# Two-phase MLPs in seven half-size products, with the activations kept in DRAM between the phases

## The chip, the cores and the metric

One core of a Trainium2 chip runs the whole program in one launch. The metric is the device time in microseconds (us), 2476.63 as the median of three runs (2475.12 to 2477.98). Engine names are those of the profile: PE is TensorE, DVE is VectorE, ACT is ScalarE, POOL is GpSimd, SP is SyncE, which only issues DMAs here.

## The reference

Two layers (gated linear attention, then sliding-window attention), each followed by the same kind of MLP, for 1024 prompt tokens and 64 sample tokens, which the kernel treats as 1088 columns. All values are float32. Only the two MLPs are touched by the change:

```python
D_MODEL = 1024
D_FF = 4 * D_MODEL
...
def squared_relu_mlp(h, w_up, w_down):
    return jnp.square(jax.nn.relu(h @ w_up)) @ w_down
...
        h = rms_norm(x, norm_g[i, 2])
        x = x + rms_norm(squared_relu_mlp(h, mlp_w_up[i], mlp_w_down[i]), norm_g[i, 3])
```

## The kernel before

Everything lies with features on the 128 partitions and the 1088 tokens (`T`) along the free axis; `HALF_T` is 544. Each float32 product is made of three fp32r passes: operands are split in a high part (a cast by ACT) and a low part (value minus high part, by DVE or POOL), and PE adds hi·hi, hi·lo and lo·hi (`dense`, `dense_set`). A unit of weights is 128x1024 (512 KB); SP loads it in a slot of `w_raw`, ACT writes `w_hi`, POOL writes `w_lo` over the raw values.

The MLP has 32 tiles of 128 hidden features, in eight groups of four. For each group the kernel makes the four up tiles (`up_tile`, 72 matmuls each, out of 8 tiles of `h`), takes relu, times the norm factor `keep`, squares, and multiplies by the group's rows of the down weights, adding into `y` in SBUF. In groups 1 to 6 the down product is done as Winograd's form of Strassen's scheme: the operands are cut in two by two blocks, and seven products of half size (`PRODUCTS`, A11, S3, S1, ... are the left operands, the weight sides are differences that `mix` makes) take the place of eight. One pass `p` of four makes the output tiles p and p+4 in 7 products of 12 matmuls with 272 columns each. DVE reads each product out of PSUM and adds it to `y` (`take_product`), makes the sums of activations (`add`), their low parts (`low`) and the weight differences of the next pass (`mix`). ACT casts high parts (`high_pair` for weights) and squares. POOL writes the two low parts of a pass's weights (`low_pair`: 768 and 1024 columns), each after the differences are there.

The first group of an MLP (`for b in range(NB): for j in range(FF_TILES)`) runs block by block of tokens (384, 384, 320 columns) because the norm before it (`Border`) is finished block by block meanwhile; I call it the first wave. The last group's down product runs block by block too, for the norm after it; that is the end wave. Every engine has its own queue in program order, and the order is written by hand; semaphores count what has been done.

Of the kernel before, what the change touches and what calls it, by code (L numbers as in the profile page):

```python
# [7 lines left out]
F32 = mybir.dt.float32  # L8
# [6 lines left out]
P = 128  # L15
# [51 lines left out]
class Chip:  # L67


    def __init__(self, nc, ctx, units):  # L70
        self.nc, self.ctx = nc, ctx
        self.end = (nc.sbuf_base + 31) // 32 * 32
        self.h_hi = self.place("h_hi", [P, KT, T], F32R)
        self.h_lo = self.place("h_lo", [P, KT, T], F32R)
        self.y = self.place("y", [P, KT, T])
        self.keep = self.place("keep", [P, T])
# [16 lines left out]
        self.x_dram = nc.dram_tensor("x_scratch", [P, KT, T], F32, kind="Internal").ap()  # L93

# [33 lines left out]
class WeightStream:  # L128

    def __init__(self, chip, units):
        self.chip, self.units = chip, units
        self.raw_in = [chip.sem(f"w_raw_in{s}") for s in range(SLOTS)]
# [3 lines left out]
        self.finished = 0  # L138

# [16 lines left out]

    def hi_count(self, unit):
        return unit + 1 - 4 * self.groups_before(unit)

    def up_raw_count(self, u0, i, g):  # L160

        per_group = 3 if i % 2 else 1
        return self.raw_count(u0 + i) + 2 - per_group * PAIRED.start + per_group * g

    def up_hi_count(self, u0, i, g):
        return self.hi_count(u0 + i) + 8 - 4 * PAIRED.start + 4 * g

    def pair_number(self, u0, p, g):
        return PAIRS * (self.groups_before(u0) - PAIRED.start) + p + PAIRS * g

# [3 lines left out]
    def load(self, sp, unit):  # L174

        s = unit % SLOTS
        sp.wait_ge(self.used, self.slots_before(unit) - SLOTS + 1)
        sp.dma_start(self.chip.w_raw[:, s], self.units[unit]).then_inc(self.raw_in[s], 16)

    def load_rounds(self, sp, first, end):  # L180

        extra = 4 * self.groups_before(SLOTS * first)
        with sp.Fori(first, end) as i:
            for s in range(SLOTS):
                sp.wait_ge(self.used, SLOTS * i + (s - SLOTS + 1 + extra))
                sp.dma_start(self.chip.w_raw[:, s], self.units[SLOTS * i + s]).then_inc(self.raw_in[s], 16)

    def load_groups(self, sp, u0):

        self.load_rounds(sp, u0 // SLOTS + 1, u0 // SLOTS + 2)  # L190
        self.load(sp, u0 + 8)
        before, first = self.group_slots_before(u0), u0 + 9 - 8 * PAIRED.start
        with sp.Fori(PAIRED.start, PAIRED.stop) as g:
            for n in range(FF_TILES):
                s = (n + 1) % SLOTS
                sp.wait_ge(self.used, 12 * g + (before + n - SLOTS + 1))
                sp.dma_start(self.chip.w_raw[:, s], self.units[8 * g + (first + n)]).then_inc(self.raw_in[s], 16)
            for p in range(PAIRS):
                s = self.pair_slots(p)[0]
                sp.wait_ge(self.used, 12 * g + (before + FF_TILES + 2 * p - SLOTS + 1))  # L200
                sp.dma_start(self.chip.w_raw[:, s], self.units[8 * g + (first + FF_TILES + p)]).then_inc(self.raw_in[s], 16)
        for unit in range(u0 + 8 * PAIRED.stop + 1, u0 + MLP_UNITS):
            self.load(sp, unit)

    def group_slots_before(self, u0):
        return self.slots_before(u0) + 9 - 12 * PAIRED.start

    def pair_slots(self, p):

        return (1, 2) if p % 2 == 0 else (3, 0)  # L210

    def high_of(self, act, s, landed):
        act.wait_ge(self.raw_in[s], landed)
        self.chip.nc.scalar.copy(self.chip.w_hi[:, s], self.chip.w_raw[:, s]).then_inc(self.hi_done, 1)  # L214

    def low_of(self, pool, s, highs):
        c = self.chip
        pool.wait_ge(self.hi_done, highs)
# [3 lines left out]
    def high(self, act, unit):  # L222

        self.high_of(act, unit % SLOTS, 16 * self.raw_count(unit))

    def low(self, pool, unit):

        self.low_of(pool, unit % SLOTS, self.hi_count(unit))

    def high_up(self, act, u0, i, g):  # L230
        self.high_of(act, i, 16 * self.up_raw_count(u0, i, g))

    def low_up(self, pool, u0, i, g):
        self.low_of(pool, i, self.up_hi_count(u0, i, g))

# [2911 lines left out]
```

## Time and profile before

| what | us |
|---|---|
| median of three runs | 2476.63 |
| the profiled execution, whole | 2476.98 |
| its span, first to last instruction | 2475.2 |
| PE busy with matmuls | 2419.3 |
| DVE busy | 1240.9 |
| ACT busy | 935.3 |
| POOL busy | 626.4 |

The mean granted TensorE clock was 0.992 of full speed. The span is what the trace shows, and the whole time has 1.8 us more around it. Busy times overlap, so the engines' rows don't add up to the span; a busy PE says that a matmul was in flight, not that no cycle was lost.

### The profile page before, as it was taken

To read this page: it belongs to the slowest core of one execution; us is meant where nothing else is said; L and a number is where in the kernel's file an instruction comes from. 1 tells how busy PE (TensorE), PEld (TensorE's weight loads), DVE (VectorE), ACT (ScalarE), POOL (GpSimd) and SP (SyncE) were. 2 spreads that over 40 slices of the span, in tenths; PEclk is the share of its full clock that TensorE was granted. 3 is DMA by queue.
4 is the path that set the end of the run, shared out by engine and by line. 5 is a ranking of instruction groups with operands and counts; after the bars stand their busy time and mean duration, and the time that the engine had idled before them with its cause. 6 is when DMAs were issued, how large, how long until landed. Compare 5 with 4: busy or idle time off the path is not lost.

```text
span 2475.2 us, 45129 instructions
## 1 busy us (share of the span) xinstructions
PE 2419.3 (98%) x18094; PEld 2289.4 (92%) x18094; DVE 1240.9 (50%) x2325; ACT 935.3 (38%) x1826; POOL 626.4 (25%) x352
## 2 busy tenths in 40 slices
PE   8999999999999999999999999999999999999998
PEld 8888887799999999999999877699999999999997
DVE  6554455418245545545548344516435455445546
ACT  5454544527222232232226455536412322322222
POOL 0101020116213223322326101014313223233233
PEclk9999999999999999999999999899999999999999
DMA  3101011015111011111115100014211111111024
GB/s 113 44 18 51 19 42 41 22 47 167 60 35 60 31 45 59 42 34 59 51 47 161 62 27 19 31 35 135 75 43 44 34 59 51 34 51 59 26 80 132
DMA packets 62725, 139.03 MB, mean 56 GB/s; under 512 B 8544, under 2 KB 39520, under 8 KB 62592
## 3 DMA queue, kind: packets, MB, share of 16 engines
q1 hardware_dynamic: 54720, 130.51, 16.3%
q10 hardware_dynamic: 7808, 6.56, 0.9%
q8 instruction: 94, 1.54, 0.3%
q14 instruction: 39, 0.32, 0.0%
q0 software_dynamic: 64, 0.10, 0.0%
HBM read 117.74 MB, written 19.40 MB: 55 GB/s over the span
## 4 chain that ended last, share of the span: by engine, by line
PE 88%; DVE 6%; ACT 3%; issue 2%; ACTq 0%; POOL 0%; DVEq 0%; POOLq 0%
PE banks L326 32%; PE banks L310 22%; PE banks L1176 20%; PE banks L2242 4%; PE banks L2377 1%; PE banks L2396 1%; DVE y L753 1%; DVE norm_acc_x L713 1%; PE banks L1752 1%; PE banks L1733 1%; PE banks L1720 1%; PE banks L1760 1%; ACT banks L625 1%; PE banks L2386 1%; DVE norm_acc L702 1%
## 5 line engine op out<-in xcount | busy, mean ns | idle before, releaser
L219 POOL TENSOR_TENSOR w_lo<-w_raw,w_hi 128x1024 fp32r<-128x1024 f32 x116 | 285.5, 2466 | 1036.4 <-ACT w_hi L214 1036.0
L310 PE MATMUL banks<-h_hi,w_hi 128*128 128x384 f32 (+1 forms) x1224 | 423.3, 346 | 4.7 <-DVE h_lo L2807 2.1
L310 PE MATMUL banks<-h_lo,w_hi 128*128 128x384 f32 (+1 forms) x1224 | 404.6, 331 | 0.0
L310 PE MATMUL banks<-h_hi,w_lo 128*128 128x384 f32 (+1 forms) x1224 | 404.2, 330 | 0.0
L266 POOL TENSOR_TENSOR w_lo<-w_raw,w_hi 128x768 fp32r<-128x768 f32 x96 | 202.4, 2129 | 638.9 <-DVE w_raw L252 638.9
L1402 DVE TENSOR_TENSOR y<-banks,y 128x544 f32<-128x544 f32 x336 | 243.3, 724 | 201.8 <-PE banks L1176 197.4
L326 PE MATMUL banks<-h_hi,w_hi 128*128 128x384 f32 (+1 forms) x1368 | 301.9, 329 | 2.0 <-DVE y L1402 2.0
L326 PE MATMUL banks<-h_lo,w_hi 128*128 128x384 f32 (+1 forms) x1368 | 301.3, 328 | 0.0
L326 PE MATMUL banks<-h_hi,w_lo 128*128 128x384 f32 (+1 forms) x1368 | 301.3, 328 | 0.0
L310 PEld LDWEIGHTS banks<-h_hi,w_hi 128*128 128x128 f32 x1224 | 232.0, 190 | 27.3 <-issue 19.3
L326 PEld LDWEIGHTS banks<-h_hi,w_hi 128*128 128x128 f32 x1368 | 233.5, 188 | 2.4 <-issue 2.4
L326 PEld LDWEIGHTS banks<-h_hi,w_lo 128*128 128x128 f32 x1368 | 233.8, 188 | 0.0
L326 PEld LDWEIGHTS banks<-h_lo,w_hi 128*128 128x128 f32 x1368 | 233.7, 188 | 0.0
L310 PEld LDWEIGHTS banks<-h_lo,w_hi 128*128 128x128 f32 x1224 | 232.5, 190 | 1.3
L310 PEld LDWEIGHTS banks<-h_hi,w_lo 128*128 128x128 f32 x1224 | 231.7, 189 | 0.0
L214 ACT CAST w_hi<-w_raw 128x1024 fp32r<-128x1024 f32 x132 | 137.9, 1046 | 189.7 <-DMA w_raw<-in_units 188.8
L1176 PE MATMUL banks<-mlp_a_hi,w_hi 128*128 128x272 f32 x768 | 158.5, 288 | 0.0
L1176 PE MATMUL banks<-mlp_a_lo,w_hi 128*128 128x272 f32 x768 | 158.4, 288 | 0.0
L1176 PE MATMUL banks<-mlp_a_hi,w_lo 128*128 128x272 f32 x768 | 158.2, 288 | 0.0
L1367 DVE SCALAR_TENSOR_TENSOR mlp_a_raw<-banks,keep 128x768 f32<-128x768 f32 (+1 forms) x60 | 40.7, 720 | 209.1 <-PE banks L326 209.1
L2884 DVE COPY_PREDICATED gla_att<-gla_masks,banks 128x128 f32<-128x128 uint8 (+1 forms) x108 | 31.8, 295 | 176.5 <-PE banks L2362 174.1
L1176 PEld LDWEIGHTS banks<-mlp_a_lo,w_hi 128*128 128x128 f32 x768 | 120.3, 189 | 0.0
(238 smaller groups left out, 4481.9 us busy)
## 6 DMA issues: line engine op xcount, KB each, us to landing
w_raw<-in_units SPq DMA_DIRECT2D x180, 512.0 KB, 3.5
x_scratch<-y SPq DMA_DIRECT2D x48, 192.0 KB, 2.6
norm_x<-x_scratch SPq DMA_DIRECT2D x28, 192.0 KB, 3.3
x_scratch<-y SPq DMA_DIRECT2D x24, 160.0 KB, 1.8
norm_x<-x_scratch SPq DMA_DIRECT2D x20, 160.0 KB, 2.9
y<-in_x SPq DMA_DIRECT2D x16, 192.0 KB, 4.9
out_y<-y SPq DMA_DIRECT2D x16, 192.0 KB, 3.3
norm_x<-in_x SPq DMA_DIRECT2D x12, 192.0 KB, 3.2
```

The costliest lines, as they stand in the source:

```text
L214: self.chip.nc.scalar.copy(self.chip.w_hi[:, s], self.chip.w_raw[:, s]).then_inc(self.hi_done, 1)
L219: c.nc.gpsimd.tensor_tensor(c.w_lo[:, s], c.w_raw[:, s], c.w_hi[:, s].bitcast(F32), ALU.subtract).then_inc(self.ready, 1)
L266: c.nc.gpsimd.tensor_tensor(c.w_lo[:, s, at], c.w_raw[:, s, at], c.w_hi[:, s, at].bitcast(F32), ALU.subtract).then_inc(self.pair_ready, 1)
L310: mm = chip.nc.tensor.matmul(out, w, x, start=(first and n == 0), stop=(last and n == 2))
L326: mm = chip.nc.tensor.matmul(chip.banks[:, bank0 + b, 0:WIDTH[b]], w, x[:, k, COLS[b]], start=(k == 0 and n == 0), stop=(k == n_k - 1 and ...
L625: nc.scalar.activation(out, y, ACT.Square).then_inc(self.s.squared_x, 1)
L702: self.chip.nc.vector.tensor_tensor(acc, before, square, ALU.add).then_inc(self.s.summed, 1)
L1176: mm = nc.tensor.matmul(chip.banks[:, bank + c, 0:half], w, x[:, c * half:(c + 1) * half], start=(not prod.adds and kappa == 0 and n == 0) ...
L1367: op = nc.vector.scalar_tensor_tensor(out=out, in0=bank, scalar=0.0, in1=keep, op0=ALU.max, op1=ALU.mult)
L1402: nc.vector.tensor_tensor(y, self.slot_banks(self.PRODUCTS[i].slot), y, ALU.add).then_inc(self.prod_added, 1)
L2242: mm = nc.tensor.matmul(out, x, y, start=(k == 0 and i == 0), stop=(k == KT - 1 and i == 2))
L2884: nc.vector.copy_predicated(a, self.masks[0:n, i, 0:n], chip.banks[0:n, self.X_BANK, i * P:i * P + n]).then_inc(self.att_step if i < 2 els ...
```

## The change

Each MLP now runs in two phases. First all 32 up tiles: four in the first wave as before, two more plain ones, and 26 in 13 "doubles", each of which makes two tiles by seven half-size products of 24 matmuls (four pairs of input tiles deep). For that the sums of `h` are made in SBUF after the first wave (`sums_of_h`, with `gain` on ACT). What a double gives has to be put together by DVE (`C22_TWO` to `C21_TAKEN`), and the sums for the second phase are made at once (`sums_of_act`). Four activation blocks and three sums are stored to DRAM (`store_set`, 1088 KB and 816 KB for a set of two tiles). Then the second phase: seven groups of four passes over the stored sets, all in seven half-size products, with operands loaded back in seven pieces of 544 KB a group (`load_piece`), cast by ACT (`high_piece`) and split by DVE (`low_piece`, two halves of 544 columns). The four first tiles' down product is the end wave. Both `mix` calls of a double and the one of a pass are on DVE; POOL keeps `low_pair`. The sums overwrite what was the raw operand, and two weight units of a double lie in the memory of `y`, which is free in the first phase. The loops of DVE, ACT, POOL and SP are written out; PE's are loops over two doubles, and over two groups.

```diff
-    def tensor(self, pe): ...
+        double(0, 0, first=True)
+        with pe.Fori(1, (DOUBLES + 1) // 2) as r:
+            double(2 * r + -1, 1)
+            double(2 * r, 0)
+        down(0, 0, first=True)
+        with pe.Fori(1, (GROUPS + 1) // 2) as r:
+            down(2 * r + -1, 1)
+            down(2 * r, 0)
...
+        def down_bank(d, i):
+            before, n = {0: (1, 4), 1: (1, 5), 2: (1, 7), 3: (0, 1), 4: (0, 2), 5: (1, 6), 6: (0, 3)}[i]
+            pe.wait_ge(self.y_added, self.adds(d + -before, n))
...
+        def double_until_c21(n):
+            c22, banks, last = self.halves(self.c22[:]), self.slot_banks, n == DOUBLES - 1
+            dve.wait_ge(self.copied, self.copies(n + 1))
+            full(n, 1)
+            combine(n, self.C22_TWO, self.c22[:], banks(1), c22, ALU.add)
+            full(n, 2)
+            combine(n, self.C22_THREE, self.c22[:], banks(2), c22, ALU.add, self.C22_TWO)
+            ws.mix(dve, nc.vector, self.down_unit(0) if last else self.double_unit(n + 1, 0))
+            if last:
+                low_piece(0, 0)
+            full(n, 3)
+            dve.wait_ge(self.a_out, self.outs(n + 1))
+            nc.vector.scalar_tensor_tensor(out=self.halves(a11), in0=banks(3), scalar=0.0, in1=self.halves(keep[0]),
+                                           op0=ALU.max, op1=ALU.mult).then_inc(self.stepped, 1)
+            if last:
+                low_piece(0, 1)
+                low_piece(0, 2)
+            else:
+                ws.mix(dve, nc.vector, self.double_unit(n + 1, 1))
+            full(n, 5)
+            combine(n, self.C22_FULL, self.c22[:], banks(5), c22, ALU.add, self.C22_THREE)
+            combine(n, self.C12_RAW, a12, c22, banks(4), ALU.subtract, self.C22_FULL)
+            relu(n, a12, a12, 0, self.C12_RAW)
+            relu(n, a22, self.c22[:], 1, self.C22_FULL)
+            if last:
+                low_piece(0, 3)
+            full(n, 6)
+            combine(n, self.C21_RAW, a21, c22, banks(6), ALU.subtract)
+            relu(n, a21, a21, 1, self.C21_RAW)
...
+        for d in range(PAIRS * GROUPS):
+            g, p = divmod(d, PAIRS)
+            for i in range(self.N_PROD):
+                take_product(d, i)
+                if i == 1 and d < PAIRS * GROUPS - 1:
+                    ws.mix(dve, nc.vector, self.down_unit(d + 1))
+                if d == 0 and i < 3:
+                    low_piece(0, 4 + i)
+                if g < GROUPS - 1:
+                    piece = {(1, 2): 0, (1, 5): 1, (2, 1): 2, (2, 3): 3, (2, 5): 4, (3, 2): 5, (3, 5): 6}.get((p, i))
+                    if piece is not None:
+                        low_piece(g + 1, piece)
```

How the queue of DVE moved is best seen in its instructions. At the end of the first wave (the 320-column block) it had these before (`mlp_a_raw<-banks` takes a tile out of PSUM, `mlp_a_lo` is its low part, `y<-banks` comes from the first down product):

```order
L1354 SCALAR_TENSOR_TENSOR mlp_a_raw<-banks,keep 128x320
L1345 TENSOR_TENSOR mlp_a_lo<-mlp_a_raw,mlp_a_hi 128x384
L1354 SCALAR_TENSOR_TENSOR mlp_a_raw<-banks,keep 128x320
L1345 TENSOR_TENSOR mlp_a_lo<-mlp_a_raw,mlp_a_hi 128x320
L1354 SCALAR_TENSOR_TENSOR mlp_a_raw<-banks,keep 128x320
L1345 TENSOR_TENSOR mlp_a_lo<-mlp_a_raw,mlp_a_hi 128x320
L1354 SCALAR_TENSOR_TENSOR mlp_a_raw<-banks,keep 128x320
L1345 TENSOR_TENSOR mlp_a_lo<-mlp_a_raw,mlp_a_hi 128x320 x2
```

In the changed kernel the same place has four sums of `h` (`mlp_s_raw`) between one tile and the next:

```order
L1619 SCALAR_TENSOR_TENSOR mlp_first_act<-banks,keep 128x320
L1502 SCALAR_TENSOR_TENSOR mlp_s_raw<-y,gains,mlp_s_raw 128x544
L1504 SCALAR_TENSOR_TENSOR mlp_s_raw<-y,gains,mlp_s_raw 128x544
L1507 TENSOR_TENSOR mlp_s_raw<-mlp_s_raw 128x544
L1509 TENSOR_TENSOR mlp_s_raw<-mlp_s_raw 128x544
L1619 SCALAR_TENSOR_TENSOR mlp_first_act<-banks,keep 128x320
```

So each tile is taken out of PSUM behind the four sums of the tile before it, and the low parts of the first tiles have gone to the end of the MLP.

Before the first double, DVE has this queue (`h_lo` and `mlp_s_lo` are low parts of the sums, `mlp_act<-banks` takes a plain tile; the first product of the double is to be written in the first plain tile's PSUM banks):

```order
L240 TENSOR_TENSOR w_raw<-w_raw 128x512
L243 TENSOR_TENSOR w_raw<-w_raw 128x256
L245 TENSOR_TENSOR w_raw<-w_raw 128x256
L240 TENSOR_TENSOR wide_raw_57<-wide_raw_57 128x512
L243 TENSOR_TENSOR wide_raw_57<-wide_raw_57 128x256
L245 TENSOR_TENSOR wide_raw_57<-wide_raw_57 128x256
L1513 TENSOR_TENSOR mlp_s_lo<-mlp_s_raw,mlp_s_hi 128x1632 x4
L1542 SCALAR_TENSOR_TENSOR mlp_act<-banks,keep 128x768
L1542 SCALAR_TENSOR_TENSOR mlp_act<-banks,keep 128x320
L1513 TENSOR_TENSOR h_lo<-mlp_s_raw,h_hi 128x544 x4
L1542 SCALAR_TENSOR_TENSOR mlp_act<-banks,keep 128x768
```

Before the change there were only copies of the down product in this place:

```order
L1407 COPY y<-banks 128x768
L1407 COPY y<-banks 128x320
L1407 COPY y<-banks 128x768
L1407 COPY y<-banks 128x320
L1407 COPY y<-banks 128x768
```

What is new there is the four wide subtractions and two sets of weight differences, in front of the first plain tile's reading.

In a pass of the down phase DVE had takes of products (`y<-banks,y`) and the three weight differences (`w_raw`), with register arithmetic of the loop between:

```order
L1402 TENSOR_TENSOR y<-banks,y 128x544
L244 ISA
L245 REGISTER_ALU
L247 TENSOR_TENSOR w_raw<-w_raw 128x512
L249 ISA
L250 TENSOR_TENSOR w_raw<-w_raw 128x256
L251 REGISTER_ALU
L252 TENSOR_TENSOR w_raw<-w_raw 128x256
L1399 REGISTER_ALU
L1400 REGISTER_ALU
L1402 TENSOR_TENSOR y<-banks,y 128x544
```

In the changed kernel, from the differences of the second pass of a group (p = 1) to those of the third:

```order
L240 TENSOR_TENSOR w_raw<-w_raw 128x512
L243 TENSOR_TENSOR w_raw<-w_raw 128x256
L245 TENSOR_TENSOR w_raw<-w_raw 128x256
L1603 TENSOR_TENSOR y<-banks,y 128x544
L1513 TENSOR_TENSOR h_lo<-h_raw,h_hi 128x2x544
L1603 TENSOR_TENSOR y<-banks,y 128x544 x3
L1513 TENSOR_TENSOR h_lo<-h_raw,h_hi 128x2x544
L1603 TENSOR_TENSOR y<-banks,y 128x544 x3
L240 TENSOR_TENSOR w_raw<-w_raw 128x512
```

Two low parts of loaded pieces (`h_lo<-h_raw`) now stand between the takes, one of them two places behind the differences.

## Rows read from the trace of the kernel before

**Rows 1.** Chain that ended last, MLP 0: start us, us, what

```profile
624.07 10.57 PE banks L310 x72
...
635.27 12.24 PE banks L326 x72
647.61 96.23 PE banks L326 x576
743.85 41.94 PE banks L1176 x336
785.78 48.00 PE banks L326 x288
...
1236.45 36.24 PE banks L326 x216
1272.68 21.20 PE banks L310 x120
```

**Rows 2.** What PE waited for: us in total, times, longest

```profile
PE banks L519 <- DVE norm_acc_x L713: 3.1, 3, 1.4
```

**Rows 3.** Groups by shape, 744 to 1235 us: busy us, mean ns | idle before

```profile
L1402 DVE TENSOR_TENSOR y<-banks,y 128x544 f32<-128x544 f32 x167 | 121.0, 724 | 100.1 <-PE banks L1176 97.9
...
L266 POOL TENSOR_TENSOR w_lo<-w_raw,w_hi 128x1024 fp32r<-128x1024 f32 x23 | 55.3, 2406 | 0.0
...
L266 POOL TENSOR_TENSOR w_lo<-w_raw,w_hi 128x768 fp32r<-128x768 f32 x23 | 42.6, 1852 | 298.9 <-DVE w_raw L252 298.9
L259 ACT CAST w_hi<-w_raw 128x1024 fp32r<-128x1024 f32 x23 | 24.3, 1055 | 46.7 <-DVE w_raw L252 46.7
...
L1292 ACT CAST mlp_late_s_hi<-mlp_s_raw 128x544 fp32r<-128x544 f32 x30 | 19.5, 650 | 3.3
```

**Rows 4.** Groups by shape on DVE, 620 to 745 us

```profile
L1416 DVE TENSOR_TENSOR y<-y 128x2176 f32<-128x2176 f32 x2 | 4.8, 2424 | 0.0
```

**Rows 5.** DVE in order of time in a paired pass: start us, us, instruction

```profile
847.40 0.72 DVE L1402 TENSOR_TENSOR y<-banks,y 128x544 f32<-128x544 f32 x1 [0.77 <-PE banks L1176]
848.04 0.68 DVE L247 TENSOR_TENSOR w_raw<-w_raw 128x512 f32<-128x512 f32 x1
848.76 0.42 DVE L250 TENSOR_TENSOR w_raw<-w_raw 128x256 f32<-128x256 f32 x1
849.22 0.42 DVE L252 TENSOR_TENSOR w_raw<-w_raw 128x256 f32<-128x256 f32 x1
```

**Rows 6.** POOL in order of time, the same pass

```profile
849.81 4.22 POOL L266 TENSOR_TENSOR w_lo<-w_raw,w_hi 128x768 fp32r<-128x768 f32 x2 [6.26 <-DVE w_raw L252]
```

**Rows 7.** POOL in order of time, in the first wave

```profile
584.12 2.31 POOL L768 TENSOR_TENSOR y<-y,norm_x 128x384 f32<-128x384 f32 x2
...
590.29 2.02 POOL L768 TENSOR_TENSOR y<-y,norm_x 128x384 f32<-128x384 f32 x2 [1.91 <-DVE y L753]
...
630.15 2.40 POOL L219 TENSOR_TENSOR w_lo<-w_raw,w_hi 128x1024 fp32r<-128x1024 f32 x1 [12.11 <-ACT w_hi L214]
```

**Rows 8.** DVE in order of time, in the first wave

```profile
584.55 1.00 DVE L787 SCALAR_TENSOR_TENSOR h_lo<-y,gains,h_hi 128x384 fp32r<-128x384 f32 x1
...
595.36 0.61 DVE L787 SCALAR_TENSOR_TENSOR h_lo<-y,gains,h_hi 128x384 fp32r<-128x384 f32 x1
...
624.56 0.49 DVE L1354 SCALAR_TENSOR_TENSOR mlp_a_raw<-banks,keep 128x320 f32<-128x320 f32 x1 [1.36 <-ACT keep L648]
...
628.04 0.48 DVE L1345 TENSOR_TENSOR mlp_a_lo<-mlp_a_raw,mlp_a_hi 128x320 fp32r<-128x320 f32 x1
...
631.56 1.34 DVE L1345 TENSOR_TENSOR mlp_a_lo<-mlp_a_raw,mlp_a_hi 128x320 fp32r<-128x320 f32 x1
```

**Rows 9.** DMA issues: KB each, median us from issue to landing

```profile
w_raw<-in_units SPq DMA_DIRECT2D x180, 512.0 KB, 3.5
x_scratch<-y SPq DMA_DIRECT2D x48, 192.0 KB, 2.6
```

**Rows 10.** Stages: us, busy (x) of PE, PEld, DVE, ACT, POOL, clock, DMA share, GB/s

```profile
744.00:1236.00 492.00, 491.45 (x3455) 491.23 (x3454) 255.77 (x389) 133.85 (x159) 149.66 (x68) 1.00 0.15 47
```

More of the change, by code:

```diff
@@ L180, in load_rounds @@
     def load_rounds(self, sp, first, end):
-        extra = 4 * self.groups_before(SLOTS * first)
+        shift = self.plain(SLOTS * first) - SLOTS * first
         with sp.Fori(first, end) as i:
             for s in range(SLOTS):
-                sp.wait_ge(self.used, SLOTS * i + (s - SLOTS + 1 + extra))
+                sp.wait_ge(self.used, SLOTS * i + (s - SLOTS + 1 + shift))
                 sp.dma_start(self.chip.w_raw[:, s], self.units[SLOTS * i + s]).then_inc(self.raw_in[s], 16)
[L188 to L203, printed above, removed]
@@ new lines, in double @@
+        def double(n, parity, first=False):
+            places = ((2, 4), (5, 0))[parity]
+            weights = [(places[k // 2], k % 2) for k in range(KT // 2)]
+            pair0 = 2 * ws.pair(self.double_unit(0, 0))
+            for i in range(self.N_PROD):
+                double_bank(n, i, first)
+                if i < 2:
+                    pe.wait_ge(ws.pair_ready, 4 * n + (pair0 + i + 1))
+                if first and i == 2:
+                    pe.wait_ge(self.a_ready, self.operands(KT // 2))
+                if first and i == 1:
+                    pe.wait_ge(self.a_ready, self.operands(KT // 2 + 1))
+                steps = product(i, range(KT // 2), weights)
+                for k in steps:
+                    if i < 2 and k == 1:
+                        pe.wait_ge(ws.pair_ready, 4 * n + (pair0 + 2 + i + 1))
+                    if first and i == 1 and k < KT // 2 - 1:
+                        pe.wait_ge(self.a_ready, self.operands(KT // 2 + k + 2))
@@ new lines, in scalar @@
+        for k in range(KT // 2):
+            act.wait_ge(self.stepped, self.steps(4 * k + 4))
+            nc.scalar.copy(self.s_hi[:, self.row(k)], self.s_raw[:, self.row(k)]).then_inc(self.a_hi_done, 1)
+        for part in range(2):
+            ws.high_pair(act, self.double_unit(0, part))
+        act.wait_ge(self.stepped, self.steps(self.PLAIN_STEP + 1))
+        tiles = [self.act[:, 2 * j:2 * j + 2] for j in range(PLAIN_TILES)]
+        square(tiles[0])
+        act.wait_ge(self.prod_full, self.plains(PLAIN_TILES))
@@ L1455, in vector @@
[L1455 removed]
+                if b == NB - 1:
+                    sums_of_h(j)
+        for part in range(2):
+            ws.mix(dve, nc.vector, self.double_unit(0, part))
+        for k in range(KT // 2):
+            r = self.row(k)
+            low(self.s_lo[:, r], self.s_raw[:, r], self.s_hi[:, r], self.operands(k + 1))
+        take_plain(0)
+        for k in range(KT // 2):
+            low(self.operand(self.S3, k, chip.h_lo, None), self.s3_raw[:, k], self.operand(self.S3, k, chip.h_hi, None),
+                self.operands(KT // 2 + k + 1))
```

903 lines of the change are left out of this document (495 added, 408 removed).

## The prediction

> **What bounds the kernel now.** I read the page first: PE is busy for 2419.3 of the span's 2475.2 us (the table above). Then the chain of work that ended last, in order of time, through MLP 0 [rows 1]: from the end of the first wave (634.64) to the start of the end wave (1272.68) there are 638.0 us, nearly all in unbroken pieces of PE. MLP 1 repeats this. So only what shortens PE's own work, or makes it wait, can count. Two rates are to be seen: four up tiles (288 matmuls of 363 columns on average) take 48.00 us, 12.0 a tile; one group's down product in half-size products (336 matmuls of 272 columns) takes 41.94, 124.8 ns each. Per column both are 0.46 ns, so a half-size product costs PE what its columns say. The other engines have room on average (DVE 255.8 of 492 us in groups 1 to 6, POOL 149.7) [rows 10], and the question is when, not how much.
>
> **What PE saves.** 26 up tiles took 26 x 12.0 = 312.0 us; 13 doubles of 7 x 24 = 168 matmuls take 13 x 20.97 = 272.6. The first group's plain down product (48.0) becomes a seventh group of 41.94. The stretch from first wave to end wave is then 24.0 (two plain tiles) + 272.6 + 7 x 41.94 = 590.2 us if PE never waits, 47.8 less than now. Ahead of the stretch PE waited 1.4 us for the norm sums in each MLP [rows 2]; DVE and ACT lose a low part and a cast per tile there (about 0.5 us each, eight times), so I give that wait back too.
>
> **Prices of what is added.** A take of 544 columns is 0.724 us [rows 3]; back to back it is 0.64, since ends overlap as the next instruction's start shows [rows 5]. From 544 and 2176 columns (2.424) [rows 4] a DVE subtraction costs 1.04 ns a column and 0.16 fixed: 1.29 us for a loaded piece (1088), 1.86 for a wide one (1632). The three weight differences take 1.6 us in all (848.04 to 849.64) [rows 5]. ACT: 544 columns 0.65, 1024 1.06, so 1.11 for a piece [rows 3]. POOL's two low parts: 1.85 and 2.41 [rows 3].
>
> **Where DVE and POOL meet.** In the first wave a DVE instruction with both inputs in SBUF does not run beside one of POOL: the 320-column subtraction takes 0.48, but 1.34 at 631.56, while POOL runs from 630.15 to 632.55 [rows 7, 8]: it waits for POOL's end. The 384-column one takes 0.61 alone and 1.00 at 584.55, and POOL's pair beside it 2.31, not 2.02: DVE got in between POOL's two, and POOL waited for it [rows 7, 8]. So they take turns, and a turn can last 2.4 us. Takes (one input in PSUM) are not touched: POOL's 4.22 us pair from 849.81 [rows 6] lies beside several takes. Before the change, the paired passes had only takes beside POOL's work; now sums, relus, pieces and differences (all SBUF on SBUF) stand there. This is what I price. The Trainium skill says the same in SBUF — State Buffer, Who interferes with whom: a DVE instruction with two SBUF inputs and a GpSimd instruction that reads SBUF exclude each other for the whole instruction, whoever is first. By that rule the trace agrees; a sum that ignored it would be the second rival below.
>
> A steady pass of the down phase (p = 1 or 3). The second product is ready 3.1 us after the pass begins, differences are done at 5.5 (POOL began at 849.81, the pass at 844.27) [rows 1, 6]. ACT then casts the second weight half (1.05) and the piece (1.11): ready at 7.7. POOL started its second, long operation at 7.35 and holds DVE until 9.7; piece 1.29, then take of product 3 until 11.7. The next pass's first product wants that bank at 10.5: PE waits 1.3. With the second piece, product 2 of the next pass waits a little too: 1.5 in all. For p = 2 the piece stands right behind the differences, DVE is first, POOL waits 1.0 and then 1.1 for the second piece, and the second weight half is 0.2 late. With its takes, 0.3. A group loses 1.5 + 1.5 + 0.3 = 3.3 us; groups 1 to 5: 16.5.
>
> The last group has four pieces of first tiles and two subtractions more per pass (0.72 each, `turn_back`) in the same places: I carry the queues on in the same manner and get 7.5.
>
> Start. With W the end of the first wave: the first 320-column tile is taken at W-9.6 (624.56 + 0.49) [rows 8]. ACT squares it and makes three scaled copies (0.75 each as an estimate from the 0.65 of a cast, 0.66 in a row), done W-7.0; DVE makes four sums (2.7) and only then takes the next tile, at W-3.7, not W-6.5. Again ACT (W-1.1, cast of the first plain unit until W-0.1), POOL's low part until W+2.7, into which two of DVE's sums run (2.2 us wait), the third tile is taken at W+4.4. The plain tile needs it and begins 4.4 late (0.6 before). Later DVE makes differences (3.2), then four wide low parts (7.4) against POOL's four weight operations (8.5), in turns; the first plain tile is read behind them at W+33.0, while PE has ended both at W+28.4 and needs its banks: 4.6. Another 0.6 in the first double. Start: 9.6.
>
> The doubles. 21 us each, DVE has 12.6 of work, POOL 8.5; the tightest need is the second unit's low part at 22.5, made at about 19 to 21. No wait. It holds if the stores land: 1904 KB are issued about 4 and 6 us into a double and have to be there at 18 (22.5 less POOL's 1.85, the differences' 1.6 and the relu's 0.7). At the rate of the trace (47 GB/s at a share of 0.15, 313 at full share) [rows 10] they need 6.2 us and the fixed part: 512 KB landed in 3.5 [rows 9], 1.7 of it transfer, so 1.8. They land at about 13.
>
> Between the phases, double 12 and group 0: the pieces must be cast and split between the combining steps. Piece 0 waits for POOL (2.0), the block C21 is combined at 27.7 after the double's start while product 2 of the first pass wants its bank at 24; together products 1, 2, 4, 5, 6 of pass 0 wait 0.8 + 3.0 + 0.3 + 1.2 + 1.4. Pass 1 has the sums of the last set in front of its takes, and its weights' load stands behind a 1904 KB store and four pieces: 2.2 + 1.2 at pass 2; 1.9 at pass 3; small ones 1.7. Sum 13.7.
>
> **The sum.** Waits 9.6 + 16.5 + 13.7 + 7.5 = 47.3; the stretch is 590.2 + 47.3 = 637.5, 0.5 less than now; with 1.4 ahead of it 1.9 per MLP, 3.8 for two. Against the profiled execution's own 2476.98 (0.35 above the median of 2476.63) that is 2473.2: **2473**. The gain on PE is real, and given back in turns between DVE and POOL.
>
> **Range of this case.** Each hand-over may be off by 0.05 us and each operation by 2 to 3%; as the chains run through about ten hand-overs at each place, a stretch moves by -7 to +6 us: 2459 to 2485.
>
> **Rivals.** Turns, but seldom. The margin by which POOL's second operation starts before the piece is ready is 0.35 us. If pieces come first, the steady passes lose about 1 us a group, not 3.3, and the start and the changeover lose a third less: 2 x (14 + 8) = 44 less, 2429. For it: small margins. Against: the order of the queues gives it at each pass alike.
> No turns at all (DVE and POOL pass each other): the same chains give 2.4 at the start, about 8 at the changeover and nothing steady, 10.9 a stretch: 2 x (47.8 + 1.4 - 10.9) = 76.6 less, 2400. Against it stand the 1.34 and the 1.00 [rows 8].
> Slower, DVE bounds the down phase. A group has 28 takes (19.0), four sets of differences (6.2), seven pieces (8.8) and 5.3 of waits for POOL: 39.3 of its 45 us. It decides from 42 on; if each of POOL's eight operations holds DVE by 1 us more, DVE needs 48 us a group (39.3 + 8, and hand-overs), 2.7 more than forecast; x 7 x 2 = 38: 2511.
> Slower, stores bound the doubles. From the 192 KB store (2.6 us) [rows 9] the worst rate is 75 GB/s: 26 us for a set, a landing at 30 and not at 18, 12 us a double, 26 doubles: 2473 + 312 = 2785. With 3.8 us of gain left it decides almost as soon as it costs at all, from a landing at 18, which is 1.95 MB in 11.9 us, 164 GB/s. At 200 GB/s, weights' loads in the same queues (3.0 MB and 15 us of each 21), I get 1 us a double and 25 at the changeover: 2473 + 2 x 38 = 2549. I take the upper end, 313, because it is the rate of transfers of like packets in this trace; nothing of it was a large store.
>
> **How the numbers follow.** Forecast 0.42, seldom turns 0.22, no turns 0.08, DVE bound 0.18, stores 0.10. The range leaves out no turns (0.08) and the store case (0.10): 2429 to 2512. What can be told from no change is 0.2%, 5 us: 2471.7 to 2481.6. Of the forecast's own range about 0.4 is below, 0.35 within, 0.25 above. Faster: 0.17 + 0.22 + 0.08 = 0.47; same 0.15; slower 0.10 + 0.18 + 0.10 = 0.38.
>
> **What the changed profile would show.** PE with more matmuls but fewer columns (2184 of 272 for 1872 of 363 in the up tiles of an MLP), 124.8 ns each, in doubles of 21 us without waits; a group of the down phase 45 us, not 42, with PE waiting for `y` (the take of product 3) ahead of the first product of passes 0 and 2; piece subtractions with a mean near 2 us, not 1.29; POOL's two low parts longer than 1.85 and 2.41 where p = 2; about 4 us before the first plain tile and before the first double. It would be wrong if the down groups are 42 us (then turns are rare), or if the doubles exceed 21 us with waits for the relu of A11 (stores), or if the start or changeover costs far more than 10 and 14 us.

## The result, and the profile after

The changed kernel takes 2491.51 us (median of 4 runs, 2488.36 to 2492.13); beside it the kernel before took 2476.57. The ratio is 1.0056, 95% interval 1.004 to 1.0072: slower by about 15 us, where 2473 was forecast. That lies above the forecast's own range (2459 to 2485) and inside the wide one with the rivals (2429 to 2512); the direction was missed. The profiled execution has a span of 2490.4 us.

The chain of work that ended last in the changed kernel, pieces of PE only (start us, us, what):

```profile
667.57 263.29 PE banks L1205 x2088
...
1136.24 3.27 PE banks L1205 x24
1139.62 10.75 PE banks L1205 x84
...
1186.40 10.75 PE banks L1205 x84
...
1233.19 10.75 PE banks L1205 x84
...
1279.95 21.20 PE banks L298 x120
...
2424.24 21.20 PE banks L298 x120
```

This answers to [rows 1]. The doubles run unbroken. In the down phase the chain falls to pieces, with the same pattern every 46.8 us (1139.62, 1186.40, 1233.19), where a group's matmuls need 41.94. The end waves begin at 1279.95 and 2424.24; before they began at 1272.68 and 2409.09. So the loss is 7.3 us in the first MLP and 7.9 from there to the second end wave.

What PE waited for (us in total, times, longest), the first rows:

```profile
PE banks L1205 <- DVE y L1603: 38.3, 33, 2.2
PE banks L314 <- DVE mlp_first_act L1619: 8.6, 2, 4.3
PE banks L1205 <- DVE y L1599: 7.3, 4, 2.2
PE banks L1205 <- DVE mlp_act L1552: 6.2, 4, 2.6
...
PE banks L1205 <- DVE mlp_act L1542: 4.8, 2, 2.8
PE banks L1205 <- POOL w_lo L261: 3.1, 11, 0.4
```

The take of a product out of PSUM (`y` L1603) is the largest. The first tiles (L1619) and the plain tiles (L1542) are the start; the copies of group 0's products (L1599) and the combining steps of the last double (L1552) are the changeover. [Rows 2]'s wait for the norm sums is down from 3.1 us to 0.3.

One place of the pattern, all engines in order of time (start us, us, instruction, idle before it and what ended it). It is pass p = 1 of a group and the start of p = 2, then the two same places of p = 3:

```profile
1151.03 0.68 DVE L240 TENSOR_TENSOR w_raw<-w_raw 128x512 f32<-128x512 f32 x1
1152.67 1.05 ACT L253 CAST w_hi<-w_raw 128x1024 fp32r<-128x1024 f32 x1 [3.61 <-DVE w_raw L245]
1152.71 4.23 POOL L261 TENSOR_TENSOR w_lo<-w_raw,w_hi 128x768 fp32r<-128x768 f32 x2 [5.74 <-DVE w_raw L245]
1153.63 2.10 ACT L1397 CAST h_hi<-h_raw 128x1088 fp32r<-128x1088 f32 x2
1154.76 3.33 DVE L1513 TENSOR_TENSOR h_lo<-h_raw,h_hi 128x1088 fp32r<-128x1088 f32 x1 [1.49 <-ACT h_hi L1397]
1158.01 2.38 DVE L1603 TENSOR_TENSOR y<-banks,y 128x544 f32<-128x544 f32 x3
1158.85 0.51 PE L1205 MATMUL banks<-h_hi,w_hi 128*128 128x272 f32 x2 [1.03 <-DVE y L1603]
...
1170.85 2.03 DVE L1513 TENSOR_TENSOR mlp_s_lo<-mlp_s_raw,mlp_s_hi 128x1088 fp32r<-128x1088 f32 x1
...
1175.09 0.68 DVE L240 TENSOR_TENSOR w_raw<-w_raw 128x512 f32<-128x512 f32 x1
...
1178.81 3.33 DVE L1513 TENSOR_TENSOR mlp_s_lo<-mlp_s_raw,mlp_s_hi 128x1088 fp32r<-128x1088 f32 x1 [1.48 <-ACT mlp_s_hi L1397]
1183.01 0.52 PE L1205 MATMUL banks<-h_hi,w_hi 128*128 128x272 f32 x2 [1.70 <-DVE y L1603]
```

Read it so: DVE is idle for 1.49 us until ACT has cast the piece (1154.7). By then POOL is about 0.2 us into its second, long part (the pair lasts from 1152.71 to 1156.94, the first part about 1.85 of it, as in [rows 3]). The subtraction needs 1.28 us alone but lasts 3.33, until 1.15 us after POOL's end. Behind it stands the take of product 3, and PE waits for that take at 1158.85. This is the mechanism that the prediction named, at the place it named.

The start, `mlp_first_act` and PE's wait:

```profile
634.44 2.69 POOL L230 TENSOR_TENSOR w_lo<-w_raw,w_hi 128x1024 fp32r<-128x1024 f32 x1 [16.25 <-ACT w_hi L224]
634.97 2.75 DVE L1507 TENSOR_TENSOR mlp_s_raw<-mlp_s_raw 128x544 f32<-128x544 f32 x1
...
638.39 0.48 DVE L1619 SCALAR_TENSOR_TENSOR mlp_first_act<-banks,keep 128x320 f32<-128x320 f32 x1
...
639.02 1.25 PE L314 MATMUL banks<-h_hi,w_hi 128*128 128x384 f32 x3 [4.31 <-DVE mlp_first_act L1619]
```

A sum of 544 columns (0.72 us alone) lasts 2.75 beside POOL, which ends at 637.13. The wave's last matmul ends at 634.71 (639.02 less 4.31), and the first double starts 32.9 us later, at 667.57, against a forecast of 33.0. The second wait there was 2.0 us and not the forecast 4.6: PE ran slower behind the first one (last section) and so came later to the banks that DVE still held.

### The profile page after: what moved, and what is told of

Same layout as the page of the kernel before. It is cut to its first block, busy times and chain, and to the rows that moved or that the text cites. A ratio compares the mean times of both kernels' runs of the same rounds, so it can differ in the third digit from the quotient of the medians.

```text
span 2490.4 us, 46139 instructions
## 1 busy us (share of the span) xinstructions
PE 2366.2 (95%) x18814; PEld 2215.5 (89%) x18814; DVE 1647.9 (66%) x2637; ACT 1014.6 (41%) x1910; POOL 778.2 (31%) x412
## 4 chain that ended last, share of the span: by engine, by line
PE 67%; DVE 18%; issue 8%; ACT 5%; DMA 1%; ACTq 0%; POOL 0%; DVEq 0%; SPq 0%; POOLq 0%
PE banks L1205 28%; PE banks L298 25%; DVE y L1603 6%; PE banks L2440 4%; DVE mlp_s_lo L1513 2%; ACT w_hi L253 1%; DVE w_raw L240 1%; PE banks L2575 1%; DVE h_lo L1513 1%; PE banks L2594 1%; DVE w_raw L243 1%; PE banks L1950 1%; PE banks L1931 1%; ACT h_hi L1397 1%; PE banks L1918 1%
## 5 line engine op out<-in xcount | busy, mean ns | idle before, releaser
L261 POOL TENSOR_TENSOR w_lo<-w_raw,w_hi 128x768 fp32r<-128x768 f32 (+1 forms) x164 | 385.7, 2373 | 590.6 <-DVE w_raw L245 566.0
L298 PE MATMUL banks<-h_hi,w_hi 128*128 128x384 f32 (+1 forms) x1416 | 488.3, 345 | 3.7 <-DVE w_lo L269 1.4
L298 PE MATMUL banks<-h_lo,w_hi 128*128 128x384 f32 (+1 forms) x1416 | 468.2, 331 | 0.0
L298 PE MATMUL banks<-h_hi,w_lo 128*128 128x384 f32 (+1 forms) x1416 | 467.6, 330 | 0.0
L1205 PE MATMUL banks<-h_hi,w_hi 128*128 128x272 f32 x1312 | 277.3, 293 | 55.7 <-DVE y L1603 37.0
L1603 DVE TENSOR_TENSOR y<-banks,y 128x544 f32<-128x544 f32 x360 | 259.7, 722 | 59.9 <-PE banks L1205 42.8
L1205 PE MATMUL banks<-h_lo,w_hi 128*128 128x272 f32 x1312 | 271.9, 289 | 0.0
L1205 PE MATMUL banks<-h_hi,w_lo 128*128 128x272 f32 x1312 | 271.9, 289 | 0.0
L1205 PE MATMUL banks<-mlp_s_hi,w_hi 128*128 128x272 f32 x984 | 207.9, 293 | 10.3 <-DVE mlp_act L1552 5.3
L1205 PE MATMUL banks<-mlp_s_hi,w_lo 128*128 128x272 f32 x984 | 203.3, 289 | 0.0
L1205 PE MATMUL banks<-mlp_s_lo,w_hi 128*128 128x272 f32 x984 | 202.2, 287 | 0.0
L261 POOL TENSOR_TENSOR wide_lo<-wide_raw,wide_hi 128x768 fp32r<-128x768 f32 (+1 forms) x52 | 116.5, 2262 | 145.2 <-DVE wide_raw L245 145.2
```

The source lines that it names most:

```text
L261: self.chip.nc.gpsimd.tensor_tensor(lo[:, i, at], raw[:, i, at], hi[:, i, at].bitcast(F32), ALU.subtract).then_inc(self.pair_ready, 1)
L298: mm = chip.nc.tensor.matmul(out, w, x, start=(first and n == 0), stop=(last and n == 2))
L1205: mm = nc.tensor.matmul(chip.banks[:, bank + c, 0:half], w, x[:, c * half:(c + 1) * half], start=(not prod.adds and n_k == 0 and m == 0), ...
L1603: nc.vector.tensor_tensor(y, bank, y, ALU.add).then_inc(self.y_added, 1)
```

## The experiments

All were timed against the kernel before on the same chip (2478 to 2479 us there). The changed kernel is 1.0056 of that, some 2492.5, and differences from it below are differences from that. The first four are about the groups of the down phase.

**Cast the first piece earlier.** ACT's order alone:

```diff
+                early = {1: 0, 3: 5}.get(p) if g < GROUPS - 1 else None
                 if d < PAIRS * GROUPS - 1:
-                    ws.high_pair(act, self.down_unit(d + 1))
+                    ws.high_pair(act, self.down_unit(d + 1),
+                                 (lambda: None) if early is None else (lambda: high_piece(g + 1, early)))
                 if g < GROUPS - 1:
-                    for i in ((), (0, 1, 2), (3, 4), (5, 6))[p]:
+                    for i in ((), (1, 2), (3, 4), (6,))[p]:
                         high_piece(g + 1, i)
...
         self.chip.nc.scalar.copy(hi[:, 0, QUARTER:UNIT], raw[:, 0, QUARTER:UNIT]).then_inc(self.pair_hi, 1)
+        between()
         act.wait_ge(self.mixed, 3 * self.pair(unit) + 3)
```

> Edit: in the passes p = 1 and p = 3 of the down phase ACT casts the first loaded piece between the two casts of the weight unit, not behind both; all other queues stay. Theory (DVE waits for its turn behind POOL's second, long low part because the piece is ready about 0.3 us after that part has begun): the piece is now ready before DVE comes to it, DVE gets in between POOL's two low parts, its subtraction takes 1.3 to 2.0 us instead of 3.33, and PE's waits of 1.2 and 1.9 us for the take of product 3 disappear. A group falls from 46.8 to about 43.5 us (p = 2 keeps its 0.8, a few tenths remain elsewhere), five groups in each of two MLPs: 30 us less than the changed kernel, about 2461. Rival (DVE is simply full in the down phase, with 39 of 47 us): the work and its order are the same, the group stays above 46 us and the time at 2488 or more.

Measured: 2439.32 us, ratio 0.9835 (0.9818 to 0.9851). Moving one cast in two of four passes gives some 53 us and makes the change a gain of 1.65%. Timeline of this kernel, the place that answers to 1152.67 to 1158.85 above, and its chain:

```profile
1135.90 1.10 ACT L1398 CAST h_hi<-h_raw 128x1088 fp32r<-128x1088 f32 x1
...
1139.53 5.28 POOL L262 TENSOR_TENSOR w_lo<-w_raw,w_hi 128x768 fp32r<-128x768 f32 x2 [5.76 <-DVE w_raw L245]
...
1140.00 2.54 DVE L1516 TENSOR_TENSOR h_lo<-h_raw,h_hi 128x1088 fp32r<-128x1088 f32 x1
1142.46 2.37 DVE L1606 TENSOR_TENSOR y<-banks,y 128x544 f32<-128x544 f32 x3
```

```profile
987.86 170.24 PE banks L1206 x1356
1158.10 63.38 PE banks L1206 x504
```

DVE now arrives during POOL's first part, waits for that (1.3 us) and then goes ahead of the second: it is POOL's pair that gets longer, 5.28 for 4.23, and nobody waits for POOL. PE runs four groups unbroken, 125.5 ns a matmul, 42.2 us a group. The expected 43.5 was too high: the 0.8 us of p = 2 and the longer wait of p = 3 went too, so they were the backlog of the same late piece. The rival (DVE is simply full) falls: from 1000 to 1200 us DVE is busy 174.9 of the 200 us here, more than in the changed kernel (164.4), and PE does not wait.

**POOL's parts cut short.** `width = 32` for both low parts, `w_lo` replaced by `w_hi` in the third matmul pass, in the down phase.

> Edit: POOL's two low parts of every unit of the down phase but the first are cut to 32 columns each, and the third matmul pass of those products reads the high part of the weights in place of the low part, so the low parts of these weights are left out of the result. PE's matmuls, DVE's and ACT's instructions are the same. Theory (turns between DVE and POOL are what the groups lose): every piece subtraction takes 1.28 to 1.30 us (now up to 3.33), PE waits for nothing in the steady groups, 42.0 to 42.5 us each, so five groups give back 4.4 us each and the last one about 6: about 28 us an MLP, 56 in all, 2435. Rival A (DVE is full with its own work, turns are a side effect): pieces still end late, the group stays above 45, the time above 2475. Rival B (ACT's late cast of the piece is enough by itself): PE still waits about 1 us for the take of product 3 in p = 1 and 3, group 44 us, 2460.

Measured: 2432.25 us, ratio 0.9813 (0.9797 to 0.983). Groups by shape from 1000 to 1200 us, the piece subtractions of the changed kernel and then of this one (busy us, mean ns | idle before):

```profile
L1513 DVE TENSOR_TENSOR h_lo<-h_raw,h_hi 128x1088 fp32r<-128x1088 f32 x16 | 29.6, 1847 | 5.9 <-ACT h_hi L1397 5.9
L1513 DVE TENSOR_TENSOR mlp_s_lo<-mlp_s_raw,mlp_s_hi 128x1088 fp32r<-128x1088 f32 x12 | 26.6, 2214 | 5.9 <-ACT mlp_s_hi L1397 5.9
```

```profile
L1516 DVE TENSOR_TENSOR h_lo<-h_raw,h_hi 128x1088 fp32r<-128x1088 f32 x19 | 24.4, 1284 | 7.4 <-ACT h_hi L1400 7.4
L1516 DVE TENSOR_TENSOR mlp_s_lo<-mlp_s_raw,mlp_s_hi 128x1088 fp32r<-128x1088 f32 x15 | 19.3, 1287 | 7.4 <-ACT mlp_s_hi L1400 7.4
```

DVE still waits for ACT's cast (7.4 us, 5.9 in the changed kernel), yet each subtraction takes 1.28 and PE does not wait in the steady groups (200.0 us busy of these 200): the late cast by itself costs nothing (rival B falls), and DVE's own work fits (rival A falls). From the first double to the end wave (666.72 to 1250.97) this kernel needs 584.3 us, the earlier cast 587.6, the changed kernel 612.4. So of 28.1 us an MLP that POOL's long parts cost in this stretch, the moved cast gives back 24.8. The 28.1 are not turns alone: with short parts the low part of the weights is also ready sooner, and PE's waits for it (`w_lo` L261, 3.1 us for both MLPs above) go too.

**The differences on POOL.** This undoes one part of the change, in the down phase:

```diff
-                if i == 1 and d < PAIRS * GROUPS - 1:
-                    ws.mix(dve, nc.vector, self.down_unit(d + 1))
...
+            if d:
+                pool.wait_ge(self.prod_full, self.down_count(d - 1, 1))
+                ws.mix(pool, self.chip.nc.gpsimd, self.down_unit(d))
             ws.low_pair(pool, self.down_unit(d))
```

> Edit: the weight differences of the down phase (all units but its first) are made by POOL in front of its low parts, not by DVE; the doubles keep theirs on DVE. Estimated from POOL's rows (1.85 us for 768 columns, 2.41 for 1024) they cost POOL 1.3 + 0.7 + 0.7 = 2.8 us a pass, and DVE saves 1.6. Theory (turns): POOL's work in a pass grows from 4.3 to 7 of 10.5 us, its last part ends about half a us later than now, and the pieces wait behind it: the group is 47 to 48.5 us, the time 2495 to 2510. Rival (DVE is full): with 6.2 us less on DVE a group falls to 43 to 44 us, 2455.

Measured: 2508.2 us, ratio 1.0117 (1.0098 to 1.0136), inside the expected range. In order of time:

```profile
1155.50 1.29 POOL L240 TENSOR_TENSOR w_raw<-w_raw 128x512 f32<-128x512 f32 x1 [3.62 <-PE banks L1205]
1156.87 0.74 POOL L243 TENSOR_TENSOR w_raw<-w_raw 128x256 f32<-128x256 f32 x1
1157.69 0.74 POOL L245 TENSOR_TENSOR w_raw<-w_raw 128x256 f32<-128x256 f32 x1
1158.50 4.23 POOL L261 TENSOR_TENSOR w_lo<-w_raw,w_hi 128x768 fp32r<-128x768 f32 x2
...
1160.54 3.35 DVE L1513 TENSOR_TENSOR h_lo<-h_raw,h_hi 128x1088 fp32r<-128x1088 f32 x1 [2.86 <-ACT h_hi L1397]
```

DVE has 1.6 us less to do in a pass and the kernel is 16 us slower than the changed one: a group is 47.8 us (chain pieces at 1096.88 and 1144.69). In the down phase the differences are better left on DVE.

**Narrow pieces on DVE.** `x[:, :, 0:16]` of each half, groups 1 to 6.

> Edit: DVE subtracts only 16 columns of each half of a loaded piece in groups 1 to 6, and the products of these groups read the high part of the activations in place of the low one, so the low parts of these activations are left out. Everything else stays, order and waits too. Theory (turns): an instruction of some 0.2 us of work still waits for POOL's whole operation, so the first piece subtraction of p = 1 and p = 3 lasts about 2.2 us, not 0.2; only its own 1.1 us and the backlog of p = 2 go, and the group is about 43 us, 2455. Rival (the 3.33 us are a slower subtraction, the two engines sharing a rate, not a wait for a turn): the narrow one lasts 0.2 to 0.5 us, PE never waits for the take, group 42.0 to 42.3.

Measured: 2440.27 us, ratio 0.9839 (0.9823 to 0.9856). In order of time, and a piece of the chain:

```profile
1137.35 4.23 POOL L261 TENSOR_TENSOR w_lo<-w_raw,w_hi 128x768 fp32r<-128x768 f32 x2 [6.25 <-DVE w_raw L245]
...
1139.40 2.23 DVE L1515 TENSOR_TENSOR h_lo<-h_raw,h_hi 128x32 fp32r<-128x32 f32 x1 [1.49 <-ACT h_hi L1399]
1141.55 2.37 DVE L1606 TENSOR_TENSOR y<-banks,y 128x544 f32<-128x544 f32 x3
1143.84 0.18 DVE L1515 TENSOR_TENSOR h_lo<-h_raw,h_hi 128x32 fp32r<-128x32 f32 x1
```

```profile
1121.26 42.34 PE banks L1207 x336
```

The same instruction takes 0.18 us alone and 2.23 beside POOL, until POOL's end at 1141.58. It waits for a turn of 2.05 us; a shared rate would have given a small multiple of 0.18. That row parts the two explanations, the group does not: 42.35 us (1121.26 to 1163.62) is close to the rival's 42.0 to 42.3 and below my 43. Without the 1.1 us of its own work, the wait alone leaves the take nearly in time.

**The start.** DVE's order in the last block of the first wave:

```diff
-                if b == NB - 1:
-                    sums_of_h(j)
+                if b == NB - 1 and j:
+                    sums_of_h(j - 1)
+        sums_of_h(FIRST_TILES - 1)
```

> Edit: in the 320-column block of the first wave DVE takes a tile out of PSUM before it makes the four sums of h of the tile before it; the last tile's sums come behind the loop. Nothing else moves. Theory (the start is lost in DVE's chain: a take, then 2.4 us of ACT's square and scaled copies, then 2.9 us of sums, four times): the first plain tile starts about 0.6 us after the wave and not 4.4, the 2.4 us of ACT lie beside DVE's sums of the tile before, and the four wide low parts are done before PE needs the banks of the first plain tile. The first double starts 24.7 to 25.5 us after the end of the wave, not 33.0: about 8 us less an MLP, 16 in all, 2475. Rival (the wide low parts against POOL's weight parts, 11 us in turns, set the start): only the 2.4 us of one tile are gained, 5 us in all, 2487.

Measured: 2476.51 us, ratio 0.9992 (0.9982 to 1.0001): about 16 us less than the changed kernel. The same 33.4 us of the changed kernel, then of this one (us, busy (x) of PE, PEld, DVE, ACT, POOL, clock, DMA share, GB/s):

```profile
634.60:668.00 33.40, 27.10 (x148) 26.73 (x148) 27.65 (x25) 15.47 (x18) 16.05 (x6) 0.90 0.24 81
```

```profile
634.60:668.00 33.40, 31.64 (x201) 30.99 (x200) 30.16 (x31) 16.50 (x20) 13.13 (x5) 1.00 0.27 81
```

PE gets through 53 more matmuls, and the granted clock is 1.00, not 0.90. The first double starts 24.0 us after the wave (634.38 to 658.38), a little better than expected. What is left is two waits (0.8 and 0.9 us) in product 1 of the first double.

**The plain tile taken before the wide low parts**, on top of that.

> Edit: as in e3_take_first, and DVE also takes the first plain tile before the four wide low parts, not behind them. Theory: by then the wide low parts no longer end last, so the second edit adds nothing: 2475, within 2 us of e3_take_first. Rival (the wide low parts end last): this is faster than e3_take_first by up to 5 us an MLP.

Measured: 2479.36 us, ratio 1.0006 (0.9996 to 1.0015). As expected nothing is gained; it is 2.9 us more than the run before, more than the 2 us I allowed. That the take delays the low parts that product 1 then waits for (one gap of 2.7 us there, for POOL's `wide_lo`) is my reading of the trace, not tested alone. Behind that gap PE's clock was low for a while too: over the same 33.4 us the granted clock is 0.95, where e3_take_first has 1.00.

**Both repairs, and pieces spread over all four passes.**

> Edit: e1_cast_early and e3b_take_plain together. Theory (the losses in the groups and at the start are apart in time and add): 2439 less 16, about 2423, 2.2% below the kernel before. What is left of the 48 us an MLP that PE could save: about 11 between the phases, 8 in the last group, 3 in the doubles and the clock after the start. Rival (what is gained at the start is lost in the doubles): 2435 or more.

> Edit: the start of e3b_take_plain, and in the down phase the seven pieces of a group spread otherwise: DVE subtracts one behind product 5 of each of the four passes and one behind product 0 of the passes 1 to 3, and ACT casts the latter ahead of the weight unit. Theory (turns; all that matters is that no piece stands behind POOL's long part with a take behind it that PE waits for): groups of 42.0 to 42.3 us as with the earlier cast, so 2423, within 4 us of e9_cast_and_start; if the second piece of passes with POOL's end at 10.9 us is late, PE waits a few tenths a pass and it is 5 to 10 us more. Rival (the groups need the pieces where they were): 2440 or more.

Measured: 2427.77 (0.9799, 0.9779 to 0.9818) and 2424.51 us (0.9779, 0.9762 to 0.9795). The savings at the start and in the groups add: the earlier cast's 2439.3 less the 13.1 that this start gives (2492.5 less 2479.4) is 2426.2. The 2423 expected was worked out with 16 for the start, which only e3_take_first reached. The spread pieces do as well as the earlier cast or 3 us better.

**Onward from there.** In three steps, each with the one before:

> Edit: e8_both without the earlier take of the first plain tile, that is, the seven pieces spread over the four passes and the start of e3_take_first. The start of e3_take_first measured 2.8 us less than that of e3b_take_plain, so 2424.5 less 2 to 3: 2422, within 3 us.

> Edit: f1_spread_take, and in the last group the four first tiles are spread in the same way: one subtraction behind product 0 and one behind product 5 of the passes 1 and 2, the first of each cast by ACT ahead of the weight unit. The last group now waits 6.4 us; without a subtraction that stands behind POOL's long part with a take behind it, 2 to 3 us should be left (DVE still has two more instructions a pass for turning back the sums). 3 to 4 us less an MLP: 2415. Rival (the last group waits for DVE's sheer work, turns or not): within 2 us of f1_spread_take.

> Edit: f2b_last, and in the last double DVE makes C22, the raw C12 and the raw C21 first, with the pieces 1 and 2 between and behind them and the relus at the end (ACT's waits follow). The third product of the down phase then need not wait 2.8 us for C21. Theory (DVE has too much work at the changeover, about 19 us of it between the last products of the doubles and the second pass, so what is not waited for at product 2 is waited for at product 3): within 3 us of f2b_last. Rival (one late instruction): 2 to 3 us less an MLP, 5 less in all.

Measured: 2420.85 (0.9767, 0.9754 to 0.978), 2418.02 (0.9749, 0.9736 to 0.9763) and 2416.2 us (0.9746, 0.9732 to 0.976). The second gave 2.8, where its theory has 6 and its rival under 2: its last group has one long wait left. The third gave 1.8, within its runs (2411 to 2419) nothing clear; the rival's 5 are not seen, and as the theory of too much work at the changeover has it, the waits of 0.6 and 2.8 us at products 1 and 2 become one of 2.6 at product 3. Timeline of the second, where its last wait begins:

```profile
1227.26 2.62 POOL L230 TENSOR_TENSOR w_lo<-w_raw,w_hi 128x1024 fp32r<-128x1024 f32 x1 [0.80 <-ACT w_hi L224]
1228.27 4.97 DVE L1614 TENSOR_TENSOR y<-y 128x544 f32<-128x544 f32 x2
1230.29 2.37 POOL L230 TENSOR_TENSOR w_lo<-w_raw,w_hi 128x1024 fp32r<-128x1024 f32 x1 [0.41 <-ACT w_hi L224]
...
1233.93 0.82 PE L1205 MATMUL banks<-h_hi,w_hi 128*128 128x272 f32 x2 [3.87 <-DVE y L1606]
```

The two subtractions that turn the sums back each wait for one of POOL's low parts for the end wave. They are needed only by the end wave:

```diff
+                if g == GROUPS - 1 and p == 3 and i == 4:
+                    turn_back(2)
...
-            if g == GROUPS - 1:
+            if g == GROUPS - 1 and p != 2:
                 turn_back(p)
```

> Edit: f2_best, and the two subtractions that turn the sums back after the third pass of the last group are made after product 4 of the fourth pass has been taken, not before the takes of that pass. In f2b_last these two (0.72 us each alone) last 4.97 us together, beside POOL's low parts of the end wave's units, and PE then waits 3.9 us, the longest wait left in the last group. Theory (they wait for POOL's turn, and what waits behind them are the takes that PE needs): the wait goes, nobody needs the subtractions before the end wave, 4 us less an MLP: 2408. Rival (DVE is full there): the wait moves to the end wave, within 2 us of f2_best, 2416.

Measured: 2404.56 us, ratio 0.9699 (0.9686 to 0.9713), the fastest. That is 11.6 less than f2_best, where 8 was expected, and not all of it is the edit: from the fourth pass of the down phase to the end wave the profiled executions differ by 5.6 us in the first MLP (266.3 and 260.7, the wait of 3.9 and the slow clock behind it) and by 2.0 in the second; the other 4 lie where the kernels are alike. The pair now lasts:

```profile
1233.70 1.35 DVE L1621 TENSOR_TENSOR y<-y 128x544 f32<-128x544 f32 x2
```

```profile
975.28 260.72 PE banks L1206 x2088
1235.99 21.20 PE banks L298 x120
```

From the second product of the fourth pass of the down phase to the end wave PE does not wait once (124.9 ns a matmul), and the end wave begins at 1235.99, 36.7 us earlier than in the kernel before [rows 1].

## Why the forecast was wrong

The terms of the sum for MLP 0, with PE's starts as bounds: 942.71 for the down phase, 996.11 for its second group, 1229.80 for the last. Taken off are the matmuls without waits (24.0 for the plain tiles, 272.6 for the doubles, 41.94 a group):

| waits of PE | forecast | measured |
|---|---|---|
| start, up to the first double | 9.0 | 667.57 - 634.71 - 24.0 = 8.9 |
| within the doubles | 0.6 | 942.71 - 667.57 - 272.6 = 2.5 |
| changeover, with group 0 | 13.7 | 996.11 - 942.71 - 41.94 = 11.5 |
| groups 1 to 5 | 16.5 | 1229.80 - 996.11 - 5 x 41.94 = 24.0 |
| last group | 7.5 | 1279.95 - 1229.80 - 41.94 = 8.2 |
| sum | 47.3 | 55.1 |

The stretch is 645.2 us, not 637.5; before it was 638.0. In MLP 1 it is 644.4.

**The step that failed** is the size of one term: "A group loses 1.5 + 1.5 + 0.3 = 3.3 us; groups 1 to 5: 16.5." It measured 4.8 a group, 24.0. By the starts of the matmuls (a gap less 0.125 us a matmul), p = 1 lost 1.19 + 0.31 = 1.5, as forecast, but p = 2 lost 0.6 for 0.3 and p = 3 lost 1.86 + 0.28 = 2.1 for 1.5; and each of the six waits costs 0.1 us beyond itself (below). I carried the queues through one pass and repeated it, but p = 3 does not begin like p = 1: p = 2 leaves DVE a backlog (its last piece, 2.03 us, begins at 1170.85, when p = 3 has already started), so that the weight differences and POOL start later in the pass. They begin 3.8 us into p = 1 (1151.03 less PE's start at 1147.19) and 5.2 into p = 3 (1175.09 less 1169.86). Two MLPs: 2 x 7.5 = 15 us of the 18.5 by which I was off. In the stretches the other terms nearly cancel (start -0.1, doubles +1.9, changeover -2.2, last group +0.7 in MLP 0), and that is luck; the rest lies ahead of the first waves (Smaller, below).

**What was right.** The 47.8 us of matmuls saved: doubles of 21 us, at 125.1 ns a matmul (2062 from 672 to 930 us) where 124.8 was forecast. The mechanism and its place were right, and so were its rows (subtractions of 1.85 and 2.21 us on average, near 2), PE's waits ahead of the first product of passes 0 and 2, and the 4.3 us before the first plain tile. With POOL's parts cut short the groups run at 41.9 us, so nothing else stood behind them. The rule cited there from the Trainium skill, SBUF — State Buffer, Who interferes with whom, holds: the 0.18 us instruction that lasts 2.23 is its plainest case.

**The margin was the point.** I noted that POOL starts its long part 0.35 us before the piece is ready (it was 0.2) and gave the other side of it a chance of 0.22 and 2429 (turns, but seldom). The earlier cast shows it was a switch: some 53 us hung on it, and with it thrown the kernel came to 2439, near that rival.

**Smaller.** The 1.4 us ahead of the first wave did come back: that wave's PE has no wait. But the execution profiled lost as much in the layer before, where the granted clock was low for 10.2 us and not 6.8, so the wave ends at 634.71 as before (634.64). Between the end wave of MLP 0 and the end of the first wave of MLP 1 it took 499.9 us, not 498.4. What made these differences was not tested. The term of 0.6 us within the doubles was a wait in the first double that did not come; of the 2.5 measured there 1.7 are the clock.

**The rivals.** DVE is not the bound: it is busy 82% of the steady groups (164.4 of 200 us), and with the earlier cast 87% with PE never waiting. Stores do not bound the doubles: PE never waited for a set there, and DVE waited four times, 7.6 us in both MLPs, at no cost to PE. That there are no turns is refuted by the subtraction of 32 columns. With POOL cut short in the down phase only and the start still as it was, 2432 was measured; the forecast for no turns anywhere was 2400.

**Open.** The changeover: 11.5 us an MLP, still 8.6 in the last kernel (1235.99 less PE's start of the down phase at 933.80, less seven groups), some 1.7 of it clock; only one reordering was tried. How much of the start's remaining 2 us could go was not tried.

## What to carry to other kernels

Before work moves to DVE, list its instructions with two SBUF inputs and POOL's beside them. In every trace here such a pair takes turns, so the price of one is its own time plus the rest of POOL's instruction, and whether it is paid depends on who arrives first. If an instruction that someone waits for stands behind one whose input becomes ready just after a long POOL instruction has begun, make that input ready earlier (here one cast moved on ACT), or put the instruction behind what is waited for. Where a hand calculation shows a margin smaller than the turn, work out both sides of it; and carry the queues through all passes of a period, not one.

## What was not expected of the hardware

- The turn passes between queues: when DVE's subtraction arrives during POOL's first part it goes ahead of POOL's second, although that follows at once in POOL's queue (POOL's pair 5.28 us for 4.23); when it arrives during the second it waits for all of it.
- A matmul behind a wait takes longer to be followed: 1183.01 to the row after it at 1183.36 is 0.35 us for two matmuls, against 0.25 (1136.84 less 1136.59) between others. With six waits a group this is 0.6 us.
- The granted clock can fall after waits that look short. After the 4.31 us wait the clock is 0.50 (the lower level, 1.2 GHz), and again after the 2 us wait ahead of the first double:

```profile
637.50:644.00 6.50, 4.98 (x16) 5.01 (x17) 3.98 (x6) 3.32 (x5) 1.69 (x1) 0.50 0.57 190
668.20:671.40 3.20, 3.20 (x16) 3.20 (x15) 2.17 (x2) 2.63 (x5) 2.07 (x1) 0.50 0.54 164
672.00:930.00 258.00, 258.00 (x2062) 258.00 (x2062) 193.99 (x237) 82.48 (x111) 105.90 (x48) 1.00 0.39 143
```

  These are windows of the changed kernel. The first fall cost nothing, since DVE was later still; the second cost half of its 3.4 us. With the tiles taken first neither is there. But not every such wait is followed by a fall: behind the wait of 2.64 us at 949.24 in the changed kernel the clock is 1.00 (949.3 to 953.0), behind the same wait in f2b_last (939.53) it is 0.54 (939.5 to 943.2). What parts the two was not found; so part of what a repair at the start gives can be lost to the clock later.
